# Small products of the side work laid one by one between triples of dense products, in a fused two-layer forward pass on one Trainium2 core

## The chip, the cores and the metric

One core of a Trainium2 chip (trn2) runs the whole program in one launch. The metric is device time in microseconds (us) of one execution, the median of several. TensorE multiplies matrices, VectorE is called DVE, ScalarE is called ACT, GpSimd is POOL, and SyncE (SP) issues most loads.

## What is computed

Two blocks are applied to one sequence of 512 positions of width 2048, all in fp32. The first is a convolution branch and a recurrent branch (HGRN2) with gates; the second is dilated attention beside retention, modulated by a small product of a vector. Cut to what matters:

```python
u = rmsnorm(x, g) @ w_in                      # 12 pieces: fl, q, iv, cg, xa, bg, za, og, ga, gb
ya = b_g * causal_dwconv3(c_g * xa) * silu(za)
o = hgrn2(silu(q), kk, iv, log_f)             # 8 heads of 128, decays along the sequence
yb = rms(o) * silu(og)
m = sigmoid(ga) * (ya @ w_a_out) + sigmoid(gb) * (yb @ w_b_out)
x = x + m @ w_o
x = x + sigmoid(rmsnorm(x) @ w_ple_gate) * (p @ w_ple_proj)
x = rmsnorm(x)
mod = silu(c) @ w_ada + b_ada                 # one row of 2048 times 2048 x 6144
proj = (rms_norm(x) * (1 + scale) + shift) @ w_in_2
y = [attention(q, k, v) * silu(z), retention(q, k, v) * silu(z)]   # 8 heads, 4 heads
x = rms_norm(x + gate * (y @ w_out_2))
```

## The kernel before, in words

**Dense products.** Each weight matrix is cut into column groups of 512, named in `GROUPS`: fl, q, iv, cg, xa, bg, za for each half, then og, ga, wa, gb, wb, wo, proj, gate, and for the second block qr, kr, vr, qa, ka, va, z, out. A group has up to 16 contraction blocks of 128 rows. Two blocks are one unit, loaded by one transfer into one of four `RAW` buffers. ACT casts the unit to its high half `WH` (L345), DVE subtracts to get the low half `WL` (L359), three buffers each. TensorE (`pe_dense`, the matmul at L327) computes for every block and each of the four 128-column pieces of the group the three products high x high, low x high, high x low: a triple of 128x512 matmuls in fp32r. One step of the loop over k is four triples, 12 matmuls. For most groups an even step does both blocks of a unit for column pieces 0 and 1, an odd step for pieces 2 and 3. A group accumulates in four PSUM banks out of six; the two column pieces that come last in a group's rotation use the banks of the first two pieces of the group before, so its first step can run while these are still read, and its second step can't.

**Side work.** The other parts of the computation are written as generators, one for each engine, whose bare `yield` ends a piece. After each dense step every engine runs one piece of its queue of special work (`Turns.after_step`; in the stage of ga to gb the pace is 1.2 pieces a step). `write_out` lets all engines' programs advance until an event that one asks for has been assigned by another; the order on each engine is fixed by these programs alone. Two of the eight banks serve the special work in turn.

**The three parts that the change touches.**
- `hgrn_pe`, product() (L667): ten products a head, levels 0 to 9, one piece each, the next level one step later. Levels 0 to 7 are four matmuls (128 columns at level 0, 64 at the others), levels 8 and 9 two. The operands are fp32, and each such matmul stands as two instructions. The last one signals `side`. DVE forms the operands of a level with L793 (first, into one of two buffers, so it waits for the product of two levels before), L797, L802 and L806, and takes the product of two levels before with L777, which frees its bank; ACT takes levels 8 and 9 (L708).
- `ada_pe` (L954): for each of 12 column chunks of w_ada, DVE accumulates 16 rows (L935), then four one-column products sum over the partitions, and DVE adds the bias (L941).
- `attention_pe` (L1192): for each of 8 heads and 4 query blocks, the scores product (L1177), and one step later four transposes of 128x128 of the weights PP into a bank. ACT copies them to PT (L1232) and then runs the exponential of the next block (L1215); DVE sums it (L1281, L1284), ACT scales it (L1224), and the next transposes follow. After the fourth block one value product (L1203) reads PT. A head takes 12 pieces: transposes in pieces 4, 6, 8 and 10, the value product in 11. Four heads begin after va0 and four after va1; z8, z12, z0 and z4 follow.

At the end of a group, ACT or DVE reads its four banks after the piece of the last step: L1616 for qa, L1626 for ka and va, L1646 with DVE's L1841 for z. Each program is in order, so what stands behind a wait waits too.

Of the kernel before, what the change touches and what calls it, by code (L numbers as in the profile page):

```python
# [85 lines left out]
    assert not programs, {name: asked[name][1] for name in programs}  # L86


def to_pause(part):

    answer = None
    while True:
        try:
            q = part.send(answer)
        except StopIteration:
            return False
        if q is None:
            return True
        answer = yield q


# [5 lines left out]
class Turns:  # L107

    def __init__(self):
        self.chores, self.specials, self.pace, self.owed = deque(), deque(), 1.0, 0.0

    def piece(self, queue):
        while queue:
            if (yield from to_pause(queue[0])):
                return
            queue.popleft()

    def after_step(self):  # L120
        yield from self.piece(self.chores)
        self.owed += self.pace
        while self.owed >= 1:
            self.owed -= 1
            yield from self.piece(self.specials)

    def finish(self, queue):
        while queue:
            yield from self.piece(queue)


class Feed:
# [76 lines left out]
def build(nc, xT, pT, vec, logits, cst, masks, ident, w_in, w_a, w_b, w_o, w_gate, w_proj,  # L209
# [77 lines left out]
    def pe_dense(name, xh, xl, ready, swap=False, kmap=None, fed=False, halves=False):  # L287
        nk = NK[name]
        mine = take(4, 0, NDENSE)
        banks[name] = mine  # L290
        gone = [held[b] for b in mine]
        for i, b in enumerate(mine):
            held[b] = (free_by(name), (name, i))
        for k in range(nk):
            n = FIRST[name] + k // 2
            s = n % NSPL
            if fed and k < 2:
                work = [(k, i) for i in range(4)]
            else:
                work = [(k - k % 2 + j, i + k % 2 * 2) for i in range(2) for j in range(2)]  # L300
            for q, i in work:
                kk = kmap[q] if kmap else q
                b = mine[i]
                c = slice(i * 128, i * 128 + 128)
                if swap:
                    pairs = [(xh[:, kk, c], WH[:, s, q % 2]), (xl[:, kk, c], WH[:, s, q % 2]),
                             (xh[:, kk, c], WL[:, s, q % 2])]
                else:
                    pairs = [(WH[:, s, q % 2, c], xh[:, kk]), (WH[:, s, q % 2, c], xl[:, kk]),
                             (WL[:, s, q % 2, c], xh[:, kk])]  # L310
                for j, (l, r) in enumerate(pairs):
                    if j == 0:
                        T.wait_ge(hi, (yield hi, n))
                        T.wait_ge(xhi, (yield xhi, (ready, kk)))
                        T.wait_ge(xlo, (yield xlo, (ready, kk)))
                        if q == 0 and gone[i]:
                            T.wait_ge(gone[i][0], (yield gone[i]))
                    if j == 2:
                        T.wait_ge(lo, (yield lo, n))
                    first, final = q == 0 and j == 0, q == nk - 1 and j == 2  # L320
                    if halves:
                        nc.tensor.matmul(bank[b][:, 0:256], l, r[:, 0:256], start=first, stop=final,
                                         skip_group_check=True)
                        ins = nc.tensor.matmul(bank[b][:, 256:512], l, r[:, 256:512], start=False, stop=final,
                                               skip_group_check=True)
                    else:
                        ins = nc.tensor.matmul(bank[b][:, :], l, r, start=first, stop=final)  # L327
                    done = [(name, i)] * (j == 2 and q == nk - 1)
                    done += [("unit", n)] * (j == 2 and k % 2 == 1 and (q, i) == work[-1])
                    if done:  # L330
                        ins.then_inc(dense.sem, dense.step(*done))
            yield from pe_turns.after_step()

    made = {"hi": 0, "lo": 0, "load": 0}
# [305 lines left out]
    def hgrn_pe(i, hh):  # L640
        half = hh // 4
        kk, q = KK[:, i], Q[:, i]

        def product(lev):
            took = (act if lev > 7 else dve, ("take", hh, lev))
            b, was = special_bank(("prod", hh, lev), *took)
            if was:
                T.wait_ge(was[0], (yield was))
            if lev == 0:
                T.wait_ge(dve, (yield dve, ("kk", half, i)))  # L650
                T.wait_ge(ev_d, (yield ev_d, (("q", half), i)))
                prs = [(CH[c], CH[c], CH[c]) for c in range(4)]
            else:
                T.wait_ge(dve, (yield dve, ("xl", hh, lev)))
                if lev < 8:
                    prs = [(slice(64 * c, 64 * c + 64), CH[c], CH[c]) for c in range(4)]
                elif lev == 8:
                    prs = [(CH[0], CH[0], CH[1]), (CH[1], CH[2], CH[3])]
                else:
                    end = slice(256, 512)  # L660
                    prs = [(slice(0, 256), CH[0], end), (end, CH[1], end)]
            for n, (o, s, t) in enumerate(prs):
                l, r = (kk[:, s], q[:, t]) if lev == 0 else (XX[:, lev % 2, s], XX[:, lev % 2, t])
                dst = b[:, o]
                if 0 < lev < 8:
                    r, dst = late(r, lev), dst.rearrange("p (n x) -> p n x", x=1 << (lev - 1))
                ins = nc.tensor.matmul(dst, l, r, start=True, stop=True)  # L667
                if n == len(prs) - 1:
                    ins.then_inc(side.sem, side.step(("prod", hh, lev)))

        for lev in range(1, 10):
            yield from product(lev - 1)
            yield
        yield from product(9)
        yield
        yield
        b, was = special_bank(("av", hh), dve, ("o", hh))
        T.wait_ge(was[0], (yield was))
        b2, was = special_bank(("hn", hh), dve, (("hn", hh), "m"))
        T.wait_ge(was[0], (yield was))  # L680
        for j in range(4):
            T.wait_ge(ev_a, (yield ev_a, (("iv", half), j)))
        T.wait_ge(dve, (yield dve, ("take", hh, 7)))
        T.wait_ge(act, (yield act, ("take", hh, 9)))
        for c in range(4):
            ins = nc.tensor.matmul(b[:, 128 * c:512], VN[:, c, 128 * i:128 * i + 128], AT[:, 640 * c:512 * c + 512],  # L686
                                   start=c == 0, stop=c == 3)
            if c == 3:
                ins.then_inc(side.sem, side.step(("av", hh)))
        yield  # L690
        T.wait_ge(act, (yield act, ("osq", hh)))
        ones_sum(b2, EE[:, 0], (("hn", hh), "sum"))
        yield
        yield
# [250 lines left out]
    def ada_pe():  # L945
        yield
        for n in range(192):
            c, k = divmod(n, 16)
            if k == 15:
                b, was = special_bank(("ada", c), dve, ("mod", c))  # L950
                T.wait_ge(was[0], (yield was))
                T.wait_ge(dve, (yield dve, ("ada", n)))
                for j in range(4):
                    ins = nc.tensor.matmul(b[:, j:j + 1], ACC[:, c % 2, 128 * j:128 * j + 128], ONES[:, 0:1],  # L954
                                           start=True, stop=True)
                    if j == 3:
                        ins.then_inc(side.sem, side.step(("ada", c)))
            yield

    XT = sb("XT", [16, 512], F32, W0 + 49152)  # L960
# [208 lines left out]
    def attention_pe(h, K, Vt, left):  # L1169
# [13 lines left out]
        for i in range(4):  # L1183
            if i < 3:
                yield from scores(i + 1)
            yield
            b, was = special_bank(("at", h, i), act, ("apt", h, i))
            T.wait_ge(was[0], (yield was))
            T.wait_ge(act, (yield act, ("an", h, i)))
            T.wait_ge(ld["idn"], (yield ld["idn"], 0))  # L1190
            for c in range(4):
                ins = nc.tensor.transpose(b[:, 128 * c:128 * c + 128], PP[:, i % 2, 128 * c:128 * c + 128],  # L1192
                                          IDN[:, :])
                if c == 3:
                    ins.then_inc(side.sem, side.step(("at", h, i)))
            yield
        b, was = special_bank(("av", 8 + h), act, ("ay", h))
        T.wait_ge(was[0], (yield was))
# [836 lines left out]
```

## Time and profile before

| what | value |
| --- | --- |
| median of 3 runs | 2682.02 us (2680.28 to 2682.2) |
| the profiled execution's own time | 2683.21 us |
| its span, first to last instruction | 2680.7 us |
| mean granted TensorE clock | 0.995 |
| TensorE matmuls | 2630.7 us busy, 98%, 11628 instructions |
| TensorE weight loads | 2125.3 us busy, 79%, 11628 instructions |
| DVE | 1266.5 us busy, 47% |
| ACT | 879.6 us busy, 33% |

The matmuls' and the weight loads' busy times overlap, since matmuls are pipelined and the load of the next weights runs beside a matmul; 98% so doesn't say that nothing can be saved. A line such as "L667 PE MATMUL bank<-XX 128x64 x448" is a group of instructions: line of the program, engine, operation, output and inputs, shape, count. A time in brackets in a timeline row is the idle time of that engine before the row, with the one that ended it.

### The profile page before, as it was taken

Reading aid. Unit: us, or ns where it says so; the run is one execution under the profiler, and the core shown is the slowest. Engines: PE = TensorE matmul, PEld = TensorE weight load, DVE = VectorE, ACT = ScalarE, POOL = GpSimd, SP = SyncE. Lnnn points to the kernel's source line nnn. Section 1 sums busy time; section 2 is a strip of 40 time slices with the busy share of each in tenths; the row PEclk is TensorE's granted clock in tenths of the full one; section 3 lists DMA queues with packets and bytes.
Section 4 is the critical chain, followed back from the end, with each engine's and each line's share of the span. In section 5 each row is a group of like instructions: output and inputs, shape, how many; then the busy total and the mean of one; then the engine's idle time right before and its main releaser. Section 6 shows DMA issues by size and latency. Waiting matters only on the chain.

```text
span 2680.7 us, 28502 instructions
## 1 busy us (share of the span) xinstructions
PE 2630.7 (98%) x11628; PEld 2125.3 (79%) x11628; DVE 1266.5 (47%) x1782; ACT 879.6 (33%) x1218; POOL 98.7 (4%) x79
## 2 busy tenths in 40 slices
PE   7999999999999999999999999999999999999996
PEld 6888888888888888888888888688777777778885
DVE  7546634447424555655442353562243344443423
ACT  5633324333223222222232352332232333433331
POOL 3000000000000000000000011100000000000011
PEclk9999999999999999999999999999999999999998
DMA  5322233222234666666452232235222222222422
GB/s 179 102 79 71 79 88 101 85 73 71 87 99 131 210 208 206 198 203 208 140 168 100 80 107 97 71 104 165 87 66 68 80 78 79 72 71 87 164 94 79
DMA packets 155074, 303.84 MB, mean 113 GB/s; under 512 B 10752, under 2 KB 11008, under 8 KB 153920
## 3 DMA queue, kind: packets, MB, share of 16 engines
q1 hardware_dynamic: 154144, 300.46, 35.6%
q8 instruction: 91, 1.49, 0.2%
q0 software_dynamic: 224, 1.15, 0.1%
q10 hardware_dynamic: 576, 0.43, 0.0%
q14 instruction: 39, 0.32, 0.0%
HBM read 293.60 MB, written 8.39 MB: 113 GB/s over the span
## 4 chain that ended last, share of the span: by engine, by line
PE 93%; DVE 3%; issue 2%; ACT 1%; DMA 0%; POOL 0%; SPq 0%; ACTq 0%; DVEq 0%; POOLq 0%
PE bank L327 85%; PE bank L667 2%; PE bank L1203 1%; PE bank L1099 1%; PE bank L1177 1%; PE bank L383 1%; PE bank L686 1%; PE bank L1192 1%; PE bank L1088 1%; DVE WL L359 0%; DMA X<-in_xT 0%; DVE XL L452 0%; PE bank L954 0%; DVE X L1860 0%; ACT WH L345 0%
## 5 line engine op out<-in xcount | busy, mean ns | idle before, releaser
L327 PE MATMUL bank<-XH,WH 128*128 128x512 f32 x2816 | 1140.3, 405 | 20.2 <-DVE XL L452 11.7
L327 PE MATMUL bank<-XH,WL 128*128 128x512 f32 x2816 | 1101.2, 391 | 3.9 <-DVE WL L359 3.9
L327 PE MATMUL bank<-XL,WH 128*128 128x512 f32 x2816 | 1098.7, 390 | 0.0
L359 DVE TENSOR_TENSOR WL<-RAW,WH 128x1024 fp32r<-128x1024 f32 x436 | 537.9, 1236 | 966.4 <-ACT WH L345 965.6
L345 ACT CAST WH<-RAW 128x1024 fp32r<-128x1024 f32 x436 | 455.9, 1048 | 1206.0 <-PE bank L327 1199.3
L327 PEld LDWEIGHTS bank<-XH,WH 128*128 128x128 f32 x2816 | 530.6, 188 | 143.5 <-issue 32.9
L327 PEld LDWEIGHTS bank<-XL,WH 128*128 128x128 f32 x2816 | 531.1, 189 | 121.2 <-issue 15.8
L327 PEld LDWEIGHTS bank<-XH,WL 128*128 128x128 f32 x2816 | 529.9, 188 | 119.3 <-DVE WL L359 5.7
L327 PE MATMUL bank<-WH,XH 128*128 128x512 f32 x384 | 154.2, 402 | 0.0
L327 PE MATMUL bank<-WL,XH 128*128 128x512 f32 x384 | 149.7, 390 | 0.0
L327 PE MATMUL bank<-WH,XL 128*128 128x512 f32 x384 | 149.4, 389 | 0.0
L935 DVE SCALAR_TENSOR_TENSOR ACC<-AST,SM,ACC 128x512 f32<-128x512 f32 x180 | 134.7, 748 | 17.5 <-DMA AST<-in_w_ada 7.8
L327 PE MATMUL bank<-YH,WH 128*128 128x512 f32 x256 | 101.0, 394 | 0.0
L327 PE MATMUL bank<-YH,WL 128*128 128x512 f32 x256 | 100.5, 393 | 0.0
L327 PE MATMUL bank<-YL,WH 128*128 128x512 f32 x256 | 99.7, 389 | 0.0
L327 PEld LDWEIGHTS bank<-WH,XL 128*128 128x128 f32 x384 | 72.2, 188 | 16.9 <-issue 2.4
L327 PEld LDWEIGHTS bank<-WH,XH 128*128 128x128 f32 x384 | 72.1, 188 | 16.8 <-issue 2.4
L327 PEld LDWEIGHTS bank<-WL,XH 128*128 128x128 f32 x384 | 72.1, 188 | 15.2
L667 PEld LDWEIGHTS bank<-XX 128*128 128x128 f32 x512 | 69.4, 191 | 6.2
L667 PE MATMUL bank<-XX 128*128 128x64 f32 (+2 forms) x512 | 69.0, 275 | 0.0
L1281 DVE CUSTOM_DVE_ANT_0 PP<-PP,CM 128x512 f32<-128x512 f32 x32 | 22.1, 692 | 79.9 <-ACT PP L1215 79.9
L1232 ACT COPY PT<-bank 128x512 f32<-128x512 f32 x32 | 18.7, 585 | 116.2 <-PE bank L1192 116.2
(241 smaller groups left out, 1682.9 us busy)
## 6 DMA issues: line engine op xcount, KB each, us to landing
RAW<-in_w_in SPq DMA_DIRECT2D x304, 512.0 KB, 3.7
AST<-in_w_ada SPq DMA_DIRECT2D x192, 256.0 KB, 3.9
RAW<-in_w_o SPq DMA_DIRECT2D x32, 512.0 KB, 3.6
RAW<-in_w_gate SPq DMA_DIRECT2D x32, 512.0 KB, 3.6
RAW<-in_w_out SPq DMA_DIRECT2D x32, 512.0 KB, 3.6
RAW<-in_w_a SPq DMA_DIRECT2D x16, 512.0 KB, 4.0
RAW<-in_w_b SPq DMA_DIRECT2D x16, 512.0 KB, 4.2
XT<-in_xT SPq DMA_DIRECT2D x4, 1024.0 KB, 6.9
```

The costliest lines, as they stand in the source:

```text
L327: ins = nc.tensor.matmul(bank[b][:, :], l, r, start=first, stop=final)
L345: nc.scalar.copy(WH[:, m % NSPL], RAW[:, m % NRAW]).then_inc(hi.sem, hi.step(m))
L359: nc.vector.tensor_tensor(WL[:, m % NSPL], RAW[:, m % NRAW], WH[:, m % NSPL].bitcast(F32), ALU.subtract).then_inc(lo.sem, lo.step(m))
L383: ins = nc.tensor.matmul(out[:, :], ONES[:, :], src, start=start, stop=stop)
L667: ins = nc.tensor.matmul(dst, l, r, start=True, stop=True)
L686: ins = nc.tensor.matmul(b[:, 128 * c:512], VN[:, c, 128 * i:128 * i + 128], AT[:, 640 * c:512 * c + 512], start=c == 0, stop=c == 3)
L935: nc.vector.scalar_tensor_tensor(out=ACC[:, u], in0=AST[:, s], scalar=CA[:, k:k + 1], in1=ACC[:, u], op0=ALU.mult, op1=ALU.add).then_inc(d ...
L1088: nc.tensor.matmul(b[:, :], YY[:, 9 + 2 * r, 128 * c:128 * c + 128], YY[:, 8 + 2 * r], start=True, stop=True).then_inc(side.sem, side.step ...
L1099: ins = nc.tensor.matmul(b[:, :], V2[:, c, 256 * r + 128 * u:256 * r + 128 * u + 128], PT[:, c], start=c == 0, stop=c == 3)
L1177: nc.tensor.matmul(b[:, :], YY[:, h, 128 * i:128 * i + 128], K[:, j], start=True, stop=True).then_inc(side.sem, side.step(("as", h, i)))
L1192: ins = nc.tensor.transpose(b[:, 128 * c:128 * c + 128], PP[:, i % 2, 128 * c:128 * c + 128], IDN[:, :])
L1203: ins = nc.tensor.matmul(b[:, :], Vt[:, c, 128 * j:128 * j + 128], PT[:, c], start=c == 0, stop=c == 3)
```

## The change

A piece may now also yield `SOON`: it is not finished, but the dense work may go on. `Turns` notes that such a piece is open. `pe_dense` calls `between()` after each triple but the last of a step; this lets an open piece go on to its next `SOON` or to its end. `after_step` closes an open piece before it begins another. The three parts above yield `SOON` after each of their small products but the last. So the first product of a piece stands where it stood, after the last triple of a step, and the others stand one by one behind the next triples. Only TensorE's program changes; the signal stays on a piece's last product. No wait is added or removed.

```diff
+SOON = "soon"
@@ to_pause
         if q is None:
             return True
+        if q is SOON:
+            return SOON
@@ class Turns
     def __init__(self):
         self.chores, self.specials, self.pace, self.owed = deque(), deque(), 1.0, 0.0
+        self.open = False
 
     def piece(self, queue):
+        self.open = False
         while queue:
-            if (yield from to_pause(queue[0])):
+            paused = yield from to_pause(queue[0])
+            if paused:
+                self.open = paused is SOON
                 return
             queue.popleft()
 
+    def between(self):
+        if self.open:
+            yield from self.piece(self.specials)
+
+    def close(self):
+        while self.open:
+            yield from self.between()
+
     def after_step(self):
+        yield from self.close()
         yield from self.piece(self.chores)
         self.owed += self.pace
         while self.owed >= 1:
             self.owed -= 1
+            yield from self.close()
             yield from self.piece(self.specials)
 
     def finish(self, queue):
         while queue:
             yield from self.piece(queue)
+        self.open = False
@@ pe_dense, after the three matmuls of a triple
+                if (q, i) != work[-1]:
+                    yield from pe_turns.between()
             yield from pe_turns.after_step()
@@ hgrn_pe, product
                 if n == len(prs) - 1:
                     ins.then_inc(side.sem, side.step(("prod", hh, lev)))
+                else:
+                    yield SOON
@@ ada_pe
                     if j == 3:
                         ins.then_inc(side.sem, side.step(("ada", c)))
+                    else:
+                        yield SOON
@@ attention_pe
                 if c == 3:
                     ins.then_inc(side.sem, side.step(("at", h, i)))
+                else:
+                    yield SOON
```

## Rows read from the trace of the kernel before

**Rows 1.** The page's chain of work that ended last, by line.
```profile
PE bank L327 85%; PE bank L667 2%; PE bank L1203 1%; PE bank L1099 1%; PE bank L1177 1%; PE bank L383 1%; PE bank L686 1%; PE bank L1192 1%; PE bank L1088 1%; DVE WL L359 0%; DMA X<-in_xT 0%; DVE XL L452 0%; PE bank L954 0%; DVE X L1860 0%;
```

**Rows 2.** Groups of TensorE by shape: count, busy us, mean ns, idle before.
```profile
L667 PE MATMUL bank<-XX 128*128 128x64 f32 x448 | 55.9, 267 | 0.0
L667 PE MATMUL bank<-Q,KK 128*128 128x128 f32 x64 | 8.6, 278 | 0.0
L954 PE MATMUL bank<-ONES,ACC 128*128 128x1 f32 x96 | 11.6, 242 | 1.2 <-DVE ACC L935 1.2
L1192 PE MATMUL bank<-IDN,PP 128*128 128x128 f32 x128 | 19.2, 273 | 2.1 <-ACT PP L1224 2.1
```

**Rows 3.** Timeline around a level product: start us, duration us, engine, instruction.
```profile
305.11 1.09 PEld L667 LDWEIGHTS bank<-XX 128*128 128x128 f32 x8
305.33 1.00 PE L667 MATMUL bank<-XX 128*128 128x64 f32 x8
...
306.11 0.19 PEld L327 LDWEIGHTS bank<-XH,WH 128*128 128x128 f32 x1
...
306.23 0.19 PEld L327 LDWEIGHTS bank<-XL,WH 128*128 128x128 f32 x1
...
306.46 0.19 PEld L327 LDWEIGHTS bank<-XH,WL 128*128 128x128 f32 x1
```

**Rows 4.** Who waited for whom: us in total, times, longest us.
```profile
ACT PT L1232 <- PE bank L1192: 116.2, 32, 5.1
...
PE bank L1192 <- ACT PP L1224: 2.1, 2, 1.0
...
PE bank L327 <- DVE Y L1841: 1.5, 2, 1.2
```

**Rows 5.** Timeline from the end of group ka1.
```profile
2208.35 0.60 PE L1192 MATMUL bank<-IDN,PP 128*128 128x128 f32 x4
...
2208.99 0.58 ACT L1232 COPY PT<-bank 128x512 f32<-128x512 f32 x1 [3.91 <-PE bank L1192]
...
2210.09 2.04 ACT L1626 COPY KB<-bank 128x512 f32<-128x512 f32 x4
...
2212.94 0.76 ACT L1224 ACTIVATE PP<-PP,SS 128x512 f32<-128x512 f32 x1
...
2214.26 0.60 PE L1192 MATMUL bank<-IDN,PP 128*128 128x128 f32 x4
...
2214.89 0.58 ACT L1232 COPY PT<-bank 128x512 f32<-128x512 f32 x1 [1.20 <-PE bank L1192]
...
2217.44 0.59 PE L1203 MATMUL bank<-PT,VA 128*128 128x512 f32 x1
```

**Rows 6.** Timeline from the end of group qa1.
```profile
2153.17 0.60 PE L1192 MATMUL bank<-IDN,PP 128*128 128x128 f32 x4
...
2154.91 2.05 ACT L1616 ACTIVATE Y<-bank 128x512 f32<-128x512 f32 x4
...
2156.35 1.02 PE L1177 MATMUL bank<-KA,Y 128*128 128x512 f32 x2
```

**Rows 7.** Timeline from the end of group z8.
```profile
2319.46 0.60 PE L1192 MATMUL bank<-IDN,PP 128*128 128x128 f32 x4
...
2323.98 0.50 PE L327 MATMUL bank<-XH,WH 128*128 128x512 f32 x1 [0.32 <-DVE Y L1841]
...
2328.03 0.63 PE L1192 MATMUL bank<-IDN,PP 128*128 128x128 f32 x4 [1.03 <-ACT PP L1224]
```

**Rows 8.** Timeline in the third head's levels, group bg.
```profile
258.66 1.09 PEld L667 LDWEIGHTS bank<-XX 128*128 128x128 f32 x8
...
260.08 0.42 DVE L793 TENSOR_TENSOR XX<-Q,EE 128x256 f32<-128x256 f32 x1
...
267.14 0.43 DVE L777 COPY_PREDICATED AT<-MASK,bank 128x256 f32<-128x256 uint16 x1
...
269.58 1.09 PEld L667 LDWEIGHTS bank<-XX 128*128 128x128 f32 x8
```

## The prediction

> **What bounds the kernel now.** I read the chain of waits first: 85% of the span hangs on the dense products of L327, that is, TensorE is the bound nearly everywhere [rows 1]. Whatever puts TensorE time in or takes it out moves the end one for one, and any other engine counts only where TensorE comes to wait for it. Second, the groups by shape: the products the change touches are short but many [rows 2]. Third, the weight loads (PEld) around one piece, because they show where each slot of TensorE begins: a load starts when the matmul before it starts [rows 3]. Fourth, the waits, to find where TensorE already waits for the side work [rows 4]. Fifth, the timeline of the attention stage and of the level products, where the signal that closes a piece is used by ScalarE (ACT) and VectorE (DVE) [rows 5 to 8].
>
> **What a small product costs, in a row and alone.** In [rows 3] the load of the first small matmul starts at 305.11 and the matmul itself at 305.33, one dense slot later: that load is hidden beside the last dense matmul. The dense stream is back in step with the load at 306.23, which starts when the first dense matmul really runs. So the eight small matmuls fill 305.34 to 306.23: 0.89 us, 0.112 each. (305.34 is 305.11 plus a dense slot. A dense slot is 0.2275: in [rows 5] from 2208.35 to 2214.26 lie four transposes and 24 dense matmuls in 5.91, from 2214.26 to 2217.44 four and 12 in 3.18; the difference is 12 slots in 2.73.) The eight loads of the piece and the one after it start 0.11 apart: each small matmul is shorter than the load that runs beside it, and that load is the slot's length. Only the first load of a stretch lies beside a long matmul; but the dense load after the stretch is exposed in exchange. A stretch of n small instructions so costs n x 0.112, whatever n is. Four transposes cost 3.18 - 12 x 0.2275 = 0.45, that is, again 0.11 each.
>
> **Part 1: the split itself.** A level product or a one-column product is two instructions (the rows count 8 per piece of 4), a transpose is one. After the change a piece is 4 stretches of 2 (or of 1 for a transpose), or 2 stretches of 2 at levels 8 and 9. By the sum above, nothing is won: 4 x 2 x 0.112 is 8 x 0.112. What is added is the changeover. Extra stretches: 64 pieces of levels 0 to 7 (448 / 8 + 64 / 8, [rows 2]) x 3 = 192; 16 pieces of levels 8 and 9, x 1 = 16; 12 one-column pieces (96 / 8) x 3 = 36; 32 transposing pieces (128 / 4) x 3 = 96. Together 340. A changeover shows as no more than the 0.23 against 0.2275 of the first dense slot [rows 3] and the 0.45 against 4 x 0.112 above: between 0 and 0.01 us. I take 0.005: **+1.7 us**, ends 0 and +3.4.
>
> The Trainium skill (TensorE: Matmul & The Clock Gate, "Step-by-step: what each phase is for") says that the 64-deep queue pulls a weight load ahead of matmuls in flight when it targets the background weight buffer. Read for a single buffer this gives the +1.7; read as several loads ahead it would make this change a gain. The rows above have no load that starts before the matmul ahead of it.
>
> **Part 2: the piece's signal comes later.** Only the last product of a piece signals. Before, all four lie together; now three triples of dense products, 9 x 0.2275 = 2.05 us, lie between the first and the last. With changeovers every reader of the signal gets it 2.07 us later. Nothing of this is TensorE time by itself; it costs where the reader's chain ends last.
>
> *Attention, at the last transposes of a head.* From the first transpose at 2214.26, ACT starts the copy at 2214.89 and ends it at 2215.47; the value product (L1203) needs it and starts at 2217.44, 3.18 after the first transpose [rows 5]. With 2.07 more the copy ends at 3.28, and then comes the value product's exposed weight load of 0.11 with the semaphore: start at 3.42 instead of 3.18. 0.24 a head, 8 heads: **+1.9**, ends 0 and +2.8.
>
> *Attention, transposes that fall on the end of a dense group.* A head takes 12 pieces, its transposes are pieces 4, 6, 8 and 10, and a group has 16 steps. The piece after the last step is number 4, 8, 12, 4, 8, 12 for qa1, ka1, va1, z8, z12, z0. In four of six cases ACT stands at L1232 waiting for transposes, and behind that wait in its program are the exponential and the four reads that free the group's banks. The third and fourth column block of the next group need the first two of these banks at their second step.
> - ka1: copy 2208.99, bank reads from 2210.09 [rows 5], first bank free about 2210.7. TensorE wants it 12 dense slots and 4 transposes after 2208.35, at 2211.5. Now it is free at 2212.76 plus a load of 0.11: a stall of 1.4. The scaling L1224 ends at 2213.70, now 2215.77, with load 2215.92, against 2214.26 + 1.4: 0.3 more. **+1.7**.
> - qa1: bank reads from 2154.91, one free at 2155.5, now 2157.57. The scores product at 2156.35 (two slots of 0.43) lets the dense stream resume at 2157.21 [rows 6]: with the load, a stall of 0.45, and by the same working as above 0.35 at the next transposes: **+0.8**.
> - z8: here TensorE already waits. Its dense product stands until 2323.98 for DVE's L1841 and the next transposes until 2328.03 for L1224 [rows 7]; the list of waits shows the pattern twice, once each for z8 and z12 [rows 4]. There is no slack, the whole chain behind L1232 moves, so **+2.1**; and once more 0.4 at the transposes after it, whose exponential has a table load in front: **+0.4**.
> - z12: **+2.1**; what follows it is the last transposing piece of a head, counted above.
>
> Together 7.1; with the three second-order terms (0.3, 0.35, 0.4) gone 6.0, and that is the lower end.
>
> *Elsewhere in attention* the chain from the first transpose over copy, exponential, DVE's sum and scaling must be ready for the next transposing piece, 24 dense slots, four transposes and a scores pair or 6.8 later. In ka1 it ends 5.35 after the start, 2.04 of it bank reads [rows 5]; elsewhere so at 3.3, and 2.07 more is covered. ACT waited 116.2 us in 32 places for the transposes [rows 4]; I expect some 180. Idle time of ACT costs nothing.
>
> *Level products.* DVE's first operation of a level waits for the product of two levels before (its operand buffer), and the level ends with the taking of that product, which frees the bank. In [rows 8]: product 2's loads start at 258.66, DVE works at 260.08, and product 5 at 269.58 needs a taking that ended at 267.57, 2.01 before. This is the tightest place, in the group in which the convolution is also on DVE; with 2.07 more for the signal, product 2 closes at 261.9 and the chain behind it moves by 1.98 at most in place of the wait. Margin 0.03: I cost it at 0. What covers it is that DVE now waits for the signal; if the cover is gone, the price is a part of a weight split (1.22) each at two levels in two heads: ends 0 and +4.9.
>
> *One-column products* (twelve): DVE waits 2 us more each, 12 x 2 = 24 us in a stage of 400 us in which TensorE is the bound; SyncE's queue has the weight loads behind loads of w_ada that wait for DVE, but four units ahead, of 24 dense slots or 5.5 us each. 0.
>
> **Sum:** 1.7 + 1.9 + 7.1 = 10.7 us. The profiled execution took 2683.2 (span 2680.7), 1.2 above the median of 2682.0; against its own time that is 2693.9, and against the median **2692.7**. Ends: 0 + 0 + 6.0 = +6.0, and 3.4 + 2.8 + 7.1 + 4.9 = +18.2, so 2688.0 to 2700.2 for the forecast's own case.
>
> **Rivals.**
> - *The loads are hidden (faster).* If each extra stretch hid one load more, in the 168 extra stretches of the 64-column products (56 pieces x 3) and the 36 of the one-column products, each would win what a slot has beyond its matmul: 64 columns of fp32 stream in at most a quarter of a dense slot, 0.057, against 0.112, so 0.055 x 204 = 11 us, and as its dense load would be hidden as well, up to 22. With the signals' 9.0 still paid and no changeovers: 2680 to 2669, say 2672. It decides as soon as TensorE can have two loads ahead. Against it: nine loads in [rows 3] that keep to the matmuls' starts. 0.07.
> - *The signals are absorbed (no change).* ACT's chains may have slack that I do not see, or the banks be wanted later than I count. Only part 1 stays: 2683.7. Against it: z8 and z12, where TensorE waits already. 0.14.
> - *DVE falls behind in the levels (slower still).* Place: levels 3 to 6 of the third head of each half; decides when the margin of 0.03 is negative. 10.7 + 4.9 to 10: about 2700. 0.10.
> - *The change does not act*, since every piece is closed before the next dense triple: 2682. Against it: only the group's own step closes, after its triples. 0.02.
> - *Forecast*, 2688 to 2700: 0.67.
>
> **Numbers.** A measurement of this kernel can tell 0.2%, 5.4 us, from no change. Slower by more holds the forecast but for its lowest part, and the DVE rival: 0.73. Within it: absorbed, not acting, a few of the forecast: 0.20. Faster: 0.07. The range for 8 in 10 reaches from the absorbed case, 2683.7, to 2700.
>
> **What would show it.** The busy time of the small matmuls stays; in the loads' timeline two small slots of 0.11 stand after each triple. L1232 waits some 66 us more (32 x 2.07). TensorE waits for ACT's L1616 and L1626 at the ends of qa1 and ka1, longer for L1841, and 8 times briefly for L1232 before L1203. Wrong: small loads closer than 0.11 to a dense one; TensorE waiting for L777 or L797; or no new waits and the same time.

## The result and the profile after

The changed kernel takes 2694.57 us (median of 4 runs, 2692.68 to 2697.1), the kernel before on the same chips 2681.15 (4 runs, 2679.13 to 2682.2). The ratio is 1.0049, with a 95% interval of 1.0037 to 1.0062: slower by 13.4 us. The profiled execution has a span of 2693.2 us against 2680.7, with the same 28502 instructions, at a mean granted clock of 0.994 against 0.995.

The waits after, all engines: who waited for whom, us in total, times, longest. L327 is now L349, L954 L980, L1192 L1220, L1203 L1233, L1232 L1262, L1240 L1270, L1841 L1871.

```profile
ACT PT L1262 <- PE bank L1220: 141.8, 32, 7.1
...
DVE MOD L967 <- PE bank L980: 43.1, 12, 5.4
...
PEld bank L349 <- DVE Y L1871: 6.9, 2, 3.7
...
PE bank L349 <- DVE Y L1871: 5.6, 2, 3.2
...
PEld bank L1233 <- ACT PT L1262: 3.3, 8, 0.4
```

And of TensorE's own waits, two that are new and the one at the transposes:

```profile
PE bank L349 <- ACT KB L1656: 1.1, 1, 1.1
...
PE bank L349 <- ACT Y L1646: 0.2, 1, 0.2
PE bank L1220 <- ACT PP L1254: 0.2, 1, 0.2
```

TensorE waited 1.5 us for DVE's reads of the z banks before [rows 4] and waits 5.6 now. It waits for ACT's reads of ka (L1656) and qa (L1646), which it did not, and eight times, once a head, its weight load for the value product waits for the copy of the last transposes. Only the wait for the scaling at the transposes fell, from 2.1 [rows 4] to 0.2.

Around a level product, in the weight loads' timeline after (the answer to [rows 3]):

```profile
304.87 0.42 PEld L691 LDWEIGHTS bank<-XX 128*128 128x128 f32 x2
305.21 0.19 PEld L349 LDWEIGHTS bank<-XH,WH 128*128 128x128 f32 x1
305.32 0.19 PEld L349 LDWEIGHTS bank<-XL,WH 128*128 128x128 f32 x1
305.55 0.19 PEld L349 LDWEIGHTS bank<-XH,WL 128*128 128x128 f32 x1
305.79 0.42 PEld L691 LDWEIGHTS bank<-XX 128*128 128x128 f32 x2
...
308.55 0.19 PEld L691 LDWEIGHTS bank<-XX 128*128 128x128 f32 x1
```

Two small slots stand between the triples. From one stretch's first load to the next is 0.92 us (305.79 - 304.87): three dense slots of 0.233 and two small ones of 0.11. No load is ahead of its matmul by more than one. A step with its piece takes 308.55 - 304.87 = 3.68, where it took 3.64 before ((269.58 - 258.66) / 3, [rows 8]). The dense slots behind a small product run 0.23 to 0.24.

**Where the time went, stage by stage.** The first and the last start of a line's matmuls bound a stage. Of the kernel before (engine, operation, count: shortest, median and longest in ns, first to last start in us):

```profile
L667 PE MATMUL bank<-Q,KK x64: 271/275/377, 151.7 to 654.8; 128*128 128x128 f32 x64
```
```profile
L686 PE MATMUL bank<-AT,VN x64: 272/433/592, 190.4 to 694.8; 128*128 128x512 f32 x16, 128*128 128x384 f32 x16, 128*128 128x256 f32 x16, 128*128 128x128 f32 x16
```
```profile
L1177 PE MATMUL bank<-KA,Y x32: 591/592/592, 2101.6 to 2246.7; 128*128 128x512 f32 x32
```
```profile
L1203 PE MATMUL bank<-PT,VB x32: 591/592/593, 2300.6 to 2432.8; 128*128 128x512 f32 x32
```

And after:

```profile
L691 PE MATMUL bank<-Q,KK x64: 271/274/377, 150.5 to 657.8; 128*128 128x128 f32 x64
```
```profile
L712 PE MATMUL bank<-AT,VN x64: 272/432/592, 189.5 to 696.0; 128*128 128x512 f32 x16, 128*128 128x384 f32 x16, 128*128 128x256 f32 x16, 128*128 128x128 f32 x16
```
```profile
L1205 PE MATMUL bank<-KA,Y x32: 591/592/593, 2103.3 to 2252.1; 128*128 128x512 f32 x32
```
```profile
L1233 PE MATMUL bank<-PT,VB x32: 592/592/697, 2306.6 to 2445.4; 128*128 128x512 f32 x32
```

The level stage, first level product to last value product, took 694.8 - 151.7 = 543.1 and takes 545.5: +2.4. The attention stage, first scores to last value product, took 2432.8 - 2101.6 = 331.2 and takes 342.1: +10.9. The loads of the one-column products went from 894.4 to 1305.6 before and go from 895.7 to 1310.0: 3.1 more, of which 2.05 is only that the last one now stands three triples later, so +1.05. Together 14.35; the first level product comes 1.2 earlier and the stretches outside the three stages together take 0.65 less, which gives the span's 12.5.

### The profile page after: what moved, and what is told of

It is laid out like the page before. It is cut to its first block, busy times and chain, and to the rows that moved or that the text cites. A ratio compares the mean times of both kernels' runs of the same rounds, so it can differ in the third digit from the quotient of the medians.

```text
span 2693.2 us, 28502 instructions
## 1 busy us (share of the span) xinstructions
PE 2640.6 (98%) x11628; PEld 2121.9 (79%) x11628; DVE 1267.1 (47%) x1782; ACT 881.1 (33%) x1218; POOL 98.8 (4%) x79
## 4 chain that ended last, share of the span: by engine, by line
PE 93%; DVE 3%; issue 2%; ACT 1%; DMA 0%; POOL 0%; SPq 0%; ACTq 0%; DVEq 0%; POOLq 0%
PE bank L349 84%; PE bank L691 2%; PE bank L1233 1%; PE bank L1127 1%; PE bank L1205 1%; PE bank L407 1%; PE bank L712 1%; DVE WL L383 1%; DVE XL L476 1%; PE bank L1220 1%; PE bank L1116 1%; DMA X<-in_xT 0%; DVE X L1890 0%; ACT WH L369 0%; ACT L64 0%
## 5 line engine op out<-in xcount | busy, mean ns | idle before, releaser
L349 PE MATMUL bank<-XH,WH 128*128 128x512 f32 x2816 | 1166.9, 414 | 23.3 <-DVE XL L476 10.6
L349 PE MATMUL bank<-XH,WL 128*128 128x512 f32 x2816 | 1103.0, 392 | 4.1 <-DVE WL L383 4.1
L349 PE MATMUL bank<-XL,WH 128*128 128x512 f32 x2816 | 1101.9, 391 | 0.0
L349 PEld LDWEIGHTS bank<-XH,WH 128*128 128x128 f32 x2816 | 531.9, 189 | 144.3 <-issue 31.5
L349 PEld LDWEIGHTS bank<-XH,WL 128*128 128x128 f32 x2816 | 530.6, 188 | 119.0 <-DVE WL L383 5.8
L349 PEld LDWEIGHTS bank<-XL,WH 128*128 128x128 f32 x2816 | 532.6, 189 | 108.9 <-issue 15.6
L349 PE MATMUL bank<-WH,XH 128*128 128x512 f32 x384 | 155.8, 406 | 1.1 <-ACT KB L1656 1.1
L349 PE MATMUL bank<-WL,XH 128*128 128x512 f32 x384 | 149.7, 390 | 0.0
L349 PE MATMUL bank<-WH,XL 128*128 128x512 f32 x384 | 149.5, 389 | 0.0
L691 PEld LDWEIGHTS bank<-XX 128*128 128x128 f32 x512 | 95.9, 187 | 23.6
L349 PE MATMUL bank<-YH,WH 128*128 128x512 f32 x256 | 102.4, 400 | 0.0
L349 PE MATMUL bank<-YH,WL 128*128 128x512 f32 x256 | 100.6, 393 | 0.0
L349 PE MATMUL bank<-YL,WH 128*128 128x512 f32 x256 | 99.8, 390 | 0.0
L691 PE MATMUL bank<-XX 128*128 128x64 f32 (+2 forms) x512 | 89.1, 255 | 0.0
L349 PEld LDWEIGHTS bank<-WH,XH 128*128 128x128 f32 x384 | 72.2, 188 | 19.7 <-issue 2.4
L349 PEld LDWEIGHTS bank<-WH,XL 128*128 128x128 f32 x384 | 72.2, 188 | 16.2 <-issue 2.4
L349 PEld LDWEIGHTS bank<-WL,XH 128*128 128x128 f32 x384 | 72.1, 188 | 15.2
L1262 ACT COPY PT<-bank 128x512 f32<-128x512 f32 x32 | 18.8, 587 | 141.8 <-PE bank L1220 141.8
```

## The experiments

A changeover is the passage from dense to small products and back, once for each stretch of small products; the split adds 340 of them. Two theories. **Signal:** the cost is the piece's later signal where ACT's or DVE's chain ends last, all of it in attention, and the changeovers are a small rest. **Changeover:** each of the 340 extra stretches costs alike. Rivals beside them: the later signal costs in the levels too; the cost is wherever transposes are split. All times below are read from the rows named above, so that the length of the attention stage (before: 331.2) or of the levels stands for a few tenths of a microsecond, where the whole time stands only for some 3: four kernels that leave attention alone or move it without cost (e2, e3, e8, e9) have 331.2 or 331.3. The exception is a passage at the lower clock (last section).

**e1_attention**: the `yield SOON` of `product` and of `ada_pe` are taken out.

```diff
@@ product, ada_pe
-                else:
-                    yield SOON
```

> Only the transposes are split, level and one-column products lie together as before. Signal theory (the cost is the piece's later signal, where ACT's chain ends last): TensorE stands for the copy before each value product (8 times), for the bank reads and the next transposes at the ends of qa1, ka1, z8 and z12: +10 to +12 us. Changeover theory (each of the 340 extra stretches costs the same, 13.4 / 340 = 0.039): 96 x 0.039 = +3.8 us.

2691.54 us against 2681.71, ratio 1.0034 (1.0021 to 1.0047), +9.8. Attention 2099.8 to 2441.8, 342.0: the same 10.8 as with the whole change; levels 543.0, unchanged. Attention alone carries three quarters of the loss; the changeover theory (+3.8) falls.

**e2_levels**: only the level products are split.

```diff
@@ ada_pe, attention_pe
-                    else:
-                        yield SOON
```

> Only the level products are split. Signal theory: no waits there, only the changeovers, 208 extra stretches of about 0.015: +3 us. Changeover theory: 208 x 0.039 = +8 us. Theory that DVE falls behind in the levels: TensorE waits for L777 or L797.

2683.13, ratio 1.0007 (0.9998 to 1.0017), +1.4, which the whole time can't tell from nothing. The stage can: 150.6 to 696.1, 545.5, +2.4 as in the whole change, or 0.012 for each of 208 stretches. TensorE waits for neither L777 nor L797 (L803 and L823 in this kernel).

**e8_levels_late**: is that 2.4 the changeover or the later signal? The products of a level lie together, but where the change has the last one.

```diff
@@ product
             b, was = special_bank(("prod", hh, lev), *took)
+            for _ in range(3 if lev < 8 else 1):
+                yield SOON
```

> Nothing is split; the products of a level lie together, but where the change has the last one (behind the third triple, at levels 8 and 9 behind the first). Signal theory and changeovers: 0, within 0.5 us in the trace, since DVE has a step in hand. If the later signal costs in the levels: +3 us.

2680.72, ratio 0.9997 (0.9988 to 1.0006). Value product of the first head to that of the last: 189.3 to 693.0, 503.7, against 504.4 before and 506.5 after the change. A signal 2.05 us later costs nothing in the levels; the stretch is even 0.7 shorter, a little outside the half microsecond that was allowed, and no run shows why. The clock is at full speed throughout the levels in all three. The 2.4 is changeovers.

**e3_ada**: only the one-column products.

```diff
@@ product, attention_pe
-                else:
-                    yield SOON
```

> Only the one-column products are split. Signal theory: 36 changeovers of 0.015, +0.5 us, and DVE waits 24 us more without anyone waiting for it. Changeover theory: +1.4.

One execution, 2680.97 against 2682.01, in which a cost of 1 us can't be seen. The loads go from 893.4 to 1307.6, 414.2, +1.0 after the 2.05 of position, and the clock is at full speed in this stage here, before and after. That is 0.03 a stretch, twice what was expected and over twice as much as in the levels. No run shows why.

**e4_attention_late**: nothing is split; the four transposes lie together behind the third triple.

```diff
@@ attention_pe
+            for _ in range(3):
+                yield SOON
             T.wait_ge(was[0], (yield was))
             T.wait_ge(act, (yield act, ("an", h, i)))
@@
-                else:
-                    yield SOON
```

> Nothing is split; in attention the four transposes of a piece lie together, but behind the third triple of the next step, where the change has the last one. Signal theory: the same waits as with the split transposes, +9 to +11 us, without the changeovers. Changeover theory: 0.

2689.67, ratio 1.0026 (1.0016 to 1.0036), +8.0; attention 2102.0 to 2441.5, 339.5, +8.3, a little under what was expected. Its new waits of TensorE are those of the split kernel:

```profile
PE bank L349 <- DVE Y L1867: 5.6, 2, 3.2
...
PE bank L349 <- ACT KB L1652: 1.1, 1, 1.1
```

No product is split in this kernel, and it still loses 8.3 of the 10.8: the delay alone does it. The rest, 2.5, fits two things that this kernel doesn't have: 96 changeovers (1.3 at the levels' 0.013) and e1's waits at the next transposes, where its weight loads stand 1.1 us in two places. They are absent here since these transposes are themselves later.

**e5_last_block, e7_group_ends, e6_rest**: the 32 transposing pieces in three sets: the fourth block of each head (8), those at the ends of qa1, ka1, z8 and z12 (4), and the others (20).

```diff
@@ attention_pe, e5
-                else:
+                elif i == 3:
                     yield SOON
@@ attention_pe, e7
+                elif (h, i) in ((1, 0), (2, 2), (5, 0), (6, 2)):
@@ attention_pe, e6
+                elif i < 3 and (h, i) not in ((1, 0), (2, 2), (5, 0), (6, 2)):
```

> Only the transposes of the fourth block of each head are split. Signal theory: the value product's weight load stands 0.375 us longer, 8 times, plus 24 changeovers of 0.015: +3.4 us. Changeover theory: 24 x 0.039 = +0.9.

> The transposes are split only in the four pieces at the ends of qa1, ka1, z8 and z12. Signal theory: the waits for bank reads (0.8, 1.5, and 2.05 more at z8 and z12) and at the next transposes, and two stretches at half clock: +6 to +8 us. Changeover theory: 12 x 0.039 = +0.5.

> The transposes are split in the 20 pieces that are neither a head's fourth block nor at the end of a dense group. Signal theory: ACT's chain has 1.2 us in hand there, so only 60 changeovers of 0.015: +0.9 us and no wait. Changeover theory: +2.3.

One execution each: 2684.35, 2687.99 and 2683.62 against 2680.84.

| kernel | first scores | last value product | stage | against before |
| --- | --- | --- | --- | --- |
| before | 2101.6 | 2432.8 | 331.2 | |
| e5_last_block | 2101.4 | 2434.9 | 333.5 | +2.3 |
| e7_group_ends | 2100.6 | 2438.8 | 338.2 | +7.0 |
| e6_rest | 2102.0 | 2434.5 | 332.5 | +1.3 |
| e1_attention (all) | 2099.8 | 2441.8 | 342.0 | +10.8 |

The parts add up to 10.6 of 10.8. Four pieces out of 32 make 7.0 us, 1.75 each; the 20 others make 0.065 each. The last block's eight make 2.3, of which some 0.3 are changeovers, less than the 3.4 expected: I had added the whole length by which the weight load waits (3.3 us in the eight), and the dense matmul ahead of it covers a part. e7's waits of TensorE:

```profile
PE bank L349 <- DVE Y L1867: 5.6, 2, 3.2
...
PE bank L349 <- ACT KB L1652: 1.1, 1, 1.1
PE bank L1216 <- ACT PP L1250: 1.0, 1, 1.0
```

In e6, where no wait was expected, one is new: the weight load of the transposes after z8 stands 0.57, which costs some 0.5.

**e9_early**: the opposite direction: together and one triple earlier than before.

```diff
@@ attention_pe
             if i < 3:
                 yield from scores(i + 1)
-            yield
+            for _ in range(3):
+                yield SOON
             b, was = special_bank(("at", h, i), act, ("apt", h, i))
@@ after the transposes
             yield
+            yield
```

> Nothing is split; in attention the four transposes lie together one triple (0.68 us) earlier than before, behind the third triple of the step. Signal theory: TensorE's wait for DVE's reads at z8 and z12 (about 0.9 each) falls by up to 0.68 each: -1 to -1.4 us. Changeover theory: 0.

2682.8, ratio 1.0005 (0.9995 to 1.0015), attention 2099.9 to 2431.1, 331.2: nothing. One of its ten executions took 5415.77 us, twice the others; no run shows why, and the ratio leaves it out. Its waits tell why:

```profile
PE bank L1217 <- ACT PP L1250: 3.3, 2, 1.7
...
PE bank L349 <- DVE Y L1867: 0.5, 1, 0.5
```

The wait for DVE's reads fell from 1.5 to 0.5 as expected, and the wait for the scaling rose from 2.1 to 3.3 [rows 4], since the transposes ask for it earlier. The expectation of -1 to -1.4 us was wrong: it left out that a piece moved forward also starts to wait forward.

**e10_clock**: nothing is split; the four transposes lie together, two triples later at z8, one at z12.

```diff
@@ attention_pe
+            for _ in range({(5, 0): 2, (6, 2): 1}.get((h, i), 0)):
+                yield SOON
             T.wait_ge(was[0], (yield was))
```

> Nothing is split; the transposes lie together, two triples (1.37 us) later at the end of z8, one (0.68) at the end of z12. Signal theory: TensorE stands at the bank reads 1.37 and 0.68 us longer than before, but less long than with the change, and the granted clock stays at full speed: about +2 us, in proportion to the delay. If the half-clock stretches have another cause than the longer stand, they are there too.

One execution, 2682.69 against 2682.01. Attention 2100.0 to 2433.3, 333.3, +2.1, for 1.37 + 0.68 = 2.05 of delay. The waits for DVE's reads:

```profile
PE bank L349 <- DVE Y L1867: 3.6, 2, 1.9
```

3.6 against 1.5 [rows 4]: the delay goes into this wait one for one. Busy time and granted clock in the 3.3 us behind each of the two waits (PE busy, instructions, ..., PEclk ahead of the last two numbers):

```profile
2323.70:2327.00 3.30, 3.03 (x12) 2.17 (x12) 3.27 (x8) 1.75 (x4) 0.00 (x0) 1.00 0.00 0
2381.40:2384.70 3.30, 3.06 (x12) 2.17 (x12) 3.27 (x8) 1.75 (x4) 0.00 (x0) 1.00 0.00 0
```

The clock stays at full speed here, which it does not in the changed kernel (below).

**e11_shift**: if the group ends are the place, no transposes should fall on them. The kernel before, unsplit, with one empty piece ahead of the first head on three engines.

```diff
@@ pe, act_program, dve_program, after ("va", half)
+            if not half:
+                turns.specials.append(idle(1))
             for i in range(4):
                 turns.specials.append(attention_pe(4 * half + i, K, Vt, heads))
```

> The kernel before, with one empty piece ahead of the first attention head on TensorE, ACT and DVE, so that the transposes fall on pieces 5, 7, 9, 11 and no group ends on one. Signal theory: at z8 and z12 ACT goes to the bank reads at once; TensorE's waits there (0.9 for the banks and 1.4 at the next transposes, twice) go: -3 to -4.6 us. If these waits come from the reads themselves (table load, sigmoid, multiply) and not from what stands ahead of them: 0.

2676.91 us (11 runs) against 2681.33 (21 runs), ratio 0.9983 (0.9974 to 0.9992): **faster by 4.4 us** than the kernel before, and the fastest kernel of this study. First scores and last value product:

```profile
L1177 PE MATMUL bank<-KA,Y x32: 591/592/592, 2103.2 to 2248.3; 128*128 128x512 f32 x32
```
```profile
L1203 PE MATMUL bank<-PT,VB x32: 591/592/592, 2302.2 to 2430.5; 128*128 128x512 f32 x32
```

327.3 us, -3.9. TensorE's wait for L1841 (1.5) is gone from its waits, that for L1224 is down from 2.1 to 0.4: 3.2 of the 3.9.

**e12_shift_split**: the same shift with the transposes split.

```diff
@@ pe, act_program, dve_program, after ("va", half)
+            if not half:
+                turns.specials.append(idle(1))
@@ product, ada_pe, taken out of the change
-                else:
-                    yield SOON
```

> The same empty piece, and the transposes split as in the change (level and one-column products together). Signal theory: the group-end share (7 us) is gone, what is left is the wait before the value products (2) and 96 changeovers (1.4): 3.4 us above the shifted kernel, so -1 to +0.5 us against the kernel before, and no half-clock stretch at z8 and z12. If the cost lies in the splitting wherever it is: +10 us as with the transposes split alone.

2683.29, ratio 1.0007 (0.9998 to 1.0015), +2.0 against before where the unshifted split (e1) has +9.8. The expectation, -1 to +0.5, was missed. Attention 2104.8 to 2437.9, 333.1: 8.9 less than e1, and 5.8 above e11, not 3.4. The split so costs 5.8 with the shift and 10.8 without it: keeping transposes off the group ends takes away about half of its price in attention, less than e7's 7.0. TensorE again waits once for the z banks and twice for the scaling (the other time, at z8, 0.17).

```profile
PE bank L1216 <- ACT PP L1250: 1.3, 2, 1.1
...
PE bank L349 <- DVE Y L1873: 1.2, 1, 1.2
```

Both 1.1 and 1.2 lie at z12, where the clock stays at full speed. ACT's timeline there, split (e12) and then unsplit (e11):

```profile
2376.62 0.59 ACT L1258 COPY PT<-bank 128x512 f32<-128x512 f32 x1 [3.02 <-PE bank L1216]
...
2378.80 0.72 ACT L1250 ACTIVATE PP<-PP,SS 128x512 f32<-128x512 f32 x1 [0.96 <-DVE SS L1310]
...
2380.83 2.07 ACT L1676 ACTIVATE TZ<-bank 128x512 f32<-128x512 f32 x4
```
```profile
2372.26 0.72 ACT L1224 ACTIVATE PP<-PP,SS 128x512 f32<-128x512 f32 x1 [0.96 <-DVE SS L1284]
...
2374.30 2.06 ACT L1650 ACTIVATE TZ<-bank 128x512 f32<-128x512 f32 x4
```

The transposes of the piece before the group's end signal late, the copy, the exponential and the scaling follow late, and the bank reads stand behind them in ACT's program. From the scores product at the group's end (2377.12 and 2372.63) to these reads it is 3.71 us split and 1.67 unsplit, 2.04 more: the delay of the signal. So a transposing piece one step ahead of a group's end can cost as well.

## Why the prediction was right, and where its terms were off

The sign, the mechanism and the place were right; 10.7 us were forecast, 13.4 measured, inside the range. One term was too small, and one came out right in part by luck.

*A row costs what its parts cost.* Right: the small slots are 0.11 in both kernels, and no load runs further ahead. The rival of hidden loads, and with it the wider reading of the Trainium skill's sentence on loads pulled ahead (TensorE: Matmul & The Clock Gate, "Step-by-step: what each phase is for"), has nothing in the trace; the reading for one buffer fits, with 0.11 at each small slot.

*The changeovers.* This is the term that failed: 0.005 a stretch was taken, with an upper end of 0.01, together 1.7. Measured: 2.4 in the levels (208 stretches, 0.012), 1.0 with the one-column products (36, 0.03), and about 0.8 for e6's 60 (its 1.3 less one wait of 0.5), 0.013. With 1.3 for the 96 of attention the sum is 4.8. I had read the step from two rows of hundredths, 0.23 against 0.2275, and multiplied by 340; over such a count a hundredth decides 3 us. By the stages the change costs 4.8 + 2.0 + 7.0 + 0.5 = 14.3 (the last three terms are below; e7's 12 changeovers, 0.15, are in it twice), 3.6 more than forecast, and 3.1 of these are this term.

*Value products.* +1.9 forecast; 2.3 - 0.3 = 2.0.

*Group ends.* 7.1 forecast with the 0.4 that belongs to the piece after z8; 7.0 measured in e7, and that other 0.5 in e6. Split in two: first to last KA scores went from 2246.7 - 2101.6 = 145.1 to 147.6 in e7 (2100.6 to 2248.2), so +2.5 for qa1 and ka1, as forecast (0.8 + 1.7), and 4.5 for z8 and z12, where 4.2 was forecast.

*Their composition at z8 and z12 was wrong.* I had both waits move along, the banks' by 2.1 longer and the next transposes' 1.4 as it was. The first is right: 5.6 against 1.5 for two. But in the changed kernel the second has gone, and its time is in slower dense matmuls (last section). That 4.5 came out so near 4.2 is in part luck: nothing in the prediction allowed for the clock, and what the lower clock costs is about what the lost wait gives back. e7 shows the exchange: at z8 its clock held and the wait of 1.0 stayed, at z12 the clock fell and the wait went.

*Level products.* The later signal was costed at 0 with a margin of 0.03 us; e8 shows no loss. DVE worked in the time that it had in hand.

*One-column products.* DVE waits 43.1 us for TensorE against 18.5 before; forecast were 24 more, and nobody waits for it. Right.

```profile
DVE MOD L941 <- PE bank L954: 18.5, 11, 3.3
```

*L1232.* I expected it to wait 66 us more and it waits 25.6 more (141.8 against 116.2, [rows 4]). ACT's own work before most of these waits, the exponential and the scaling, starts later by the same 2.07 us, so there the wait only moves. A part of the 25.6 comes from ACT's other wait in attention, for the value products, which shrinks by 14.4 (before, then after):

```profile
ACT Y L1240 <- PE bank L1203: 37.2, 8, 4.7
```
```profile
ACT Y L1270 <- PE bank L1233: 22.8, 8, 2.8
```

The two together grow by 11.2, about TensorE's extra time in the stage (10.9).

The three other rivals fell: absorbed (e1: 9.8), behind in the levels (e8: no loss), not acting (the timeline).

## What to carry to other kernels

Small products whose slot is set by the next weight load (0.11 us here) cost the same in a row and one by one, so spreading them gained nothing here, and cost a changeover of 0.012 to 0.03 us for each stretch. What it changes is when the last one signals: ask who waits for it, and above all what stands behind that wait in the reader's program; here the reads that free the banks for the next group did, in 4 pieces of 32, and these made 7 of 14 us. The same reading shows a gain: one empty piece, so that the long wait does not fall on a group's end, took 4.4 us off the kernel before.

## What the runs showed of the hardware beside this

Behind its longer idle times at z8 and z12 TensorE ran slower. After z8 it stands idle until 2332.21 in the changed kernel; then, in the weight loads' timeline:

```profile
2332.21 0.19 PEld L349 LDWEIGHTS bank<-XH,WH 128*128 128x128 f32 x1 [3.20 <-DVE Y L1871]
2332.31 0.19 PEld L349 LDWEIGHTS bank<-XL,WH 128*128 128x128 f32 x1
2332.60 0.33 PEld L349 LDWEIGHTS bank<-XH,WL 128*128 128x128 f32 x1
2333.03 0.33 PEld L349 LDWEIGHTS bank<-XH,WH 128*128 128x128 f32 x1
2333.46 0.33 PEld L349 LDWEIGHTS bank<-XL,WH 128*128 128x128 f32 x1
```

The dense slots are 0.43 instead of 0.23 and a load takes 0.33 instead of 0.19. The granted clock of that stretch, after and, for the same work, before:

```profile
2332.30:2335.60 3.30, 3.30 (x9) 2.55 (x10) 3.27 (x8) 1.74 (x4) 0.00 (x0) 0.52 0.00 0
```
```profile
2324.00:2327.30 3.30, 3.00 (x12) 2.16 (x12) 3.27 (x8) 1.74 (x4) 0.00 (x0) 1.00 0.00 0
```

0.52 is nearly all of the stretch at the lower of the two levels, 1.2 GHz. Some eight matmuls lose 0.2 us each, 1.6 to 1.7, and they run in time that was TensorE's wait for the next transposes (1.4 before), so that the net loss, an estimate from these two, is a few tenths. The Trainium skill (TensorE: Matmul & The Clock Gate, "What's actually happening") says that the throttled clock is the default and activity releases it; the trace agrees in kind, with 0.52 behind an idle time of 3.20. But that idle time alone did not decide it. In e7 TensorE stood as long at z8 and the clock held, while it fell at z12:

```profile
2327.50:2330.90 3.40, 3.04 (x12) 2.18 (x12) 3.37 (x8) 1.84 (x4) 0.00 (x0) 1.00 0.00 0
2386.70:2390.10 3.40, 3.40 (x10) 2.69 (x11) 3.37 (x8) 1.83 (x4) 0.00 (x0) 0.62 0.00 0
```

and in e2, behind the short wait for the accumulation near 1080 that all kernels have, it fell (first line), although it holds there in the kernel before (second):

```profile
1082.00:1088.00 6.00, 5.79 (x22) 4.76 (x23) 2.36 (x5) 0.47 (x1) 0.00 (x0) 0.72 0.68 218
```
```profile
1079.00:1085.00 6.00, 4.81 (x25) 3.79 (x24) 3.89 (x7) 0.21 (x2) 0.00 (x0) 1.00 0.55 165
```

So one execution's span carries 1 to 2 us of this, and a stage does where such a passage falls into it: the one-column stage takes 412.7 in e2, where nothing in it is split, against 411.2 before. Differences of that size between single profiles are read from a stage whose clock was the same in both.
